# Down projection of a SwiGLU as seven quarter products, with weight sums made by GpSimd beforehand

## What is computed

```python
D_MODEL = 2048; SEQ = 512; N_MEM = 256; FFN_HIDDEN = 5632

def swiglu(h, w_gu, w_down):
    g, u = jnp.split(h @ w_gu, 2, axis=-1)
    return (jax.nn.silu(g) * u) @ w_down

def reference(x, mem, positions, ...):
    h = rmsnorm(x, norm_mix_g)
    ...                       # two attention mixers, o_a and o_b
    x = x + (gates[:, :, 0] * (o_a @ w_branch_a) + gates[:, :, 1] * (o_b @ w_branch_b)) @ w_out
    x = x + memory_cross_attention(rmsnorm(x, norm_cross_g), rmsnorm(mem, norm_mem_g), w_xq, w_xkv, w_xo)
    hf = rmsnorm(x, norm_ffn_g)
    x = x + swiglu(hf, w_gu, w_down)
    return rmsnorm(x, final_norm_g)
```

## Time and profile before

| what | us |
|---|---|
| median of 3 runs (2743.96 to 2745.4) | 2745.27 |
| the profiled execution's own span | 2743.1 |
| start to the first mix matmul | 1409.7 |
| mix stage | 829.3 |
| down stage | 488.8 |
| from the last piece to the end | 15.3 |

### The profile page before, as it was taken

The page is one execution under the profiler, slowest core; times in us unless marked ns, Lnnn a source line. Parts: engine busy times, 40 slices in busy tenths (PEclk is TensorE's granted clock), DMA queues, the critical chain, the costliest instruction groups (busy, mean ns, idle before and its releaser), DMA issues.

```text
span 2743.1 us, 34950 instructions
## 1 busy us (share of the span) xinstructions
PE 2704.5 (99%) x13710; PEld 2279.2 (83%) x13710; DVE 1737.1 (63%) x1820; ACT 1017.7 (37%) x1134; POOL 766.3 (28%) x642
## 2 busy tenths in 40 slices
PE   9999999999999999999999999999999999999997
PEld 7888888888778888888788888888888888888886
DVE  6677652334653344573677767687777777777786
ACT  6555432224642232243553333333333332222224
POOL 0000000000000003330357666776667632212120
PEclk9999999999999999999999999999999999999999
DMA  6221233322222325333434444434343463444432
GB/s 239 77 85 62 83 97 99 92 84 92 77 93 92 99 77 207 93 121 109 139 109 137 132 138 132 138 101 146 127 143 127 143 238 123 161 146 137 161 125 82
DMA packets 125889, 333.29 MB, mean 121 GB/s; under 512 B 10320, under 2 KB 57424, under 8 KB 125136
## 3 DMA queue, kind: packets, MB, share of 16 engines
q1 hardware_dynamic: 119296, 309.37, 35.3%
q10 hardware_dynamic: 6480, 22.35, 2.0%
HBM read 301.27 MB, written 30.41 MB: 121 GB/s over the span
## 4 chain that ended last, share of the span: by engine, by line
PE 92%; DVE 4%; ACT 1%; DMA 1%; issue 1%; SPq 0%; DVEq 0%; ACTq 0%
PE ps L2198 16%; PE acc L1812 14%; PE acc L1814 14%; PE acc L1813 14%; PE ps L2201 8%; PE acc L1832 6%; PE acc L1834 6%; PE acc L1833 6%; PE acc L2198 3%; PE acc L2201 1%; DMA x_tokens<-x_n 1%; PE ps L1874 1%; PE ps L1863 1%; DVE w_lo L1588 1%; ACT ps L799 0%
## 5 line engine op out<-in xcount | busy, mean ns | idle before, releaser
L1101 DVE TENSOR_TENSOR w_lo<-raw,w_hi 128x1024 fp32r<-128x1024 f32 x328 | 475.9, 1456 | 274.9 <-ACT w_hi L609 274.3
L1812 PE MATMUL acc<-act_both,w_hi 128*128 128x512 f32 (+1 forms) x1536 | 591.1, 385 | 3.6 <-DVE w_lo L1101 3.1
L1814 PE MATMUL acc<-act_both,w_lo 128*128 128x512 f32 (+1 forms) x1536 | 585.3, 381 | 0.0
L1813 PE MATMUL acc<-act_both,w_hi 128*128 128x512 f32 (+1 forms) x1536 | 584.9, 381 | 0.0
L609 ACT ACTIVATE w_hi<-raw 128x1024 fp32r<-128x1024 f32 x328 | 344.3, 1055 | 553.9 <-PE acc L1814 340.7
L1812 PEld LDWEIGHTS acc<-act_both,w_hi 128*128 128x128 f32 x1536 | 289.6, 189 | 59.4 <-DVE w_lo L1101 3.7
L1814 PEld LDWEIGHTS acc<-act_both,w_lo 128*128 128x128 f32 x1536 | 289.5, 188 | 55.4
L1813 PEld LDWEIGHTS acc<-act_both,w_hi 128*128 128x128 f32 x1536 | 289.8, 189 | 54.3 <-issue 0.7
L543 POOL MEMSET mem_stat<- 128x256 f32 x1 | 0.3, 312 | 1047.1 <-DMA mem<-mem_t 1047.1
L2198 PE MATMUL ps<-t_both,w_hi 128*128 128x512 f32 x896 | 281.6, 396 | 0.5 <-DVE cg L1616 0.5
L1832 PE MATMUL acc<-act_both,w_hi 128*128 128x512 f32 x672 | 262.9, 391 | 3.1 <-DVE x L1456 3.0
(11 more groups left out here) (306 smaller groups left out, 4752.8 us busy)
## 6 DMA issues: line engine op xcount, KB each, us to landing
raw<-w_stream SPq DMA_DIRECT2D x412, 512.0 KB, 3.6
over<-w_stream SPq DMA_DIRECT2D x84, 512.0 KB, 4.4
gate_t<-cg ACTq DMA_DIRECT2D x22, 512.0 KB, 2.6
over<-gate_t SPq DMA_DIRECT2D x22, 512.0 KB, 5.3
up_t<-cu ACTq DMA_DIRECT2D x20, 512.0 KB, 2.6
over<-up_t SPq DMA_DIRECT2D x20, 512.0 KB, 6.2
x<-x_t SPq DMA_DIRECT2D x16, 512.0 KB, 8.6
x_tokens<-x_n SPq DMA_DIRECT2D x4, 1024.0 KB, 15.4
```

Of the source, the lines that this page charges most:

```text
L1101: nc.vector.tensor_tensor(w_lo[:, s, :], raw[:, s, :], f(w_hi[:, s, :]), ALU.subtract)\
L1812: nc.tensor.matmul(dst, wh, ah, start=start and k == 0, stop=False)
L1813: nc.tensor.matmul(dst, wh, al, start=False, stop=False)
L1814: last = nc.tensor.matmul(dst, wl, ah, start=False, stop=stop and k == UK - 1)
```

## The change

The down projection is cut into quarters as the mix stage already was: hidden features (22 tiles each half, so pair p is now made of tiles p and p + 22), tokens (256 each half), outputs (8 tiles each half). Seven quarter products follow each other, each of 22 units. A unit has eight output tiles with three matmuls of 256 columns, into eight half banks of PSUM, and `x` is added to at the end of each product (`down_out`). Four of the products need sums of weight quarters. GpSimd makes these in 88 steps during the two gate stages: SyncE loads a step (512 KB, rows of 1 KB), GpSimd runs four operations of 256 elements, SyncE stores the sums to DRAM (512 KB). SwiGLU is finished within the mix stage for every pair (as the inline pairs were), with the token and feature sums of the hidden tiles made by VectorE, and eight quarters of a pair are stored (1 MB). The mix stage uses half banks of 256 columns too: each weight tile pair takes three matmuls of 256 columns instead of 512 + 256 (two tiles: 6 x 256 for 2 x 512 + 2 x 256), a group is read from PSUM by VectorE with five operations instead of ten, and TensorE waits once per group for its bank set. In the last product the output tile is the outer loop, so that `x` is finished one tile after another, and GpSimd adds up the squares.

```diff
-MIXES = (FFN // P - DIRECT) // 2
+MIXES = HID_PAIRS - 1
 MIX_UNITS = 8
 U_MIX = U_FFN + 4 * DIRECT
 U_DOWN = U_MIX + MIX_UNITS * MIXES
-UNITS = U_DOWN + GROUPS * KT // 2
+DOWNS = 7
+UNITS = U_DOWN + DOWNS * HID_PAIRS
...
+SCALED = [(1, 0, 4), (1, 4, 8), (1, 8, 12), (1, 12, 16), (0, 0, 4), (0, 4, 8), (0, 8, 12), (0, 12, 14), (0, 14, 16)]
...
+Q21, Q11, Q12, Q22 = range(4)
+W_QUADS = U_DOWN
+W_LAST = W_QUADS + 4 * HID_PAIRS
...
+DOWN_PRODUCTS = ((Q11, H11), (Q12, H21), (SUM2, HT2), (SUM1, HT1), (SUM3, HT3), (SUM4, H22), (Q22, HT4))
...
+SUM_COLS = 256
+SUM_STEPS = HID_PAIRS * UK * P // SUM_COLS
+SUM_BUFS = 3
+SUM_UNITS = (range(U_DB + 8, U_SWA), range(U_DA + 8, U_OUT))
...
+        def half_bank(bank_set, i):
+            at = 4 * S * bank_set + SH * i
+            return banks[:, at:at + SH]
...
-            ring(2, U_OUT // RING + 1)
+            def sums_in_(t):
+                if t >= SUM_BUFS:
+                    sp.wait_ge(sums_out[t % SUM_BUFS], 16 * (t // SUM_BUFS))
+                k, c = divmod(t, UK * P // SUM_COLS)
+                quads = w[W_QUADS:W_LAST, :, SUM_COLS * c:SUM_COLS * (c + 1)].rearrange("(q k) p c -> k p q c", q=4)
+                sp.dma_start(sums[t % SUM_BUFS][:], quads[k]).then_inc(sums_in[t % SUM_BUFS], 16)
+            def sums_out_(t):
+                k, c = divmod(t, UK * P // SUM_COLS)
+                sp.wait_ge(down_summed, t + 1)
+                sp.dma_start(down_sums[:, k, :, SUM_COLS * c:SUM_COLS * (c + 1)].rearrange("q p c -> p q c"),
+                             sums[t % SUM_BUFS][:]).then_inc(sums_out[t % SUM_BUFS], 16)
+            def with_sums(units):
+                begun = sums_due(units[0]).start
+                for n in units:
+                    weights(n)
+                    if n == units[0]:
+                        sp.wait_ge(ps_free, 2 + 2 * PAIRS + (0 if n < U_SWA else SWA_STEPS))
+                    for t in sums_due(n):
+                        sums_in_(t)
+                        if t > begun:
+                            sums_out_(t - 1)
+                sums_out_(sums_due(units[-1]).stop - 1)
+            ring(2, SUM_UNITS[0].start // RING)
+            with_sums(SUM_UNITS[0])
+            ring(U_SWA // RING, SUM_UNITS[1].start // RING)
+            with_sums(SUM_UNITS[1])
...
+            for t in range(SUM_STEPS):
+                part = sums[t % SUM_BUFS]
+                pool.wait_ge(sums_in[t % SUM_BUFS], 16 * (t // SUM_BUFS + 1))
+                link(nc.gpsimd.tensor_tensor(part[:, SUM3, :], part[:, Q21, :], part[:, Q11, :], ALU.subtract))
+                link(nc.gpsimd.tensor_tensor(part[:, SUM1, :], part[:, Q21, :], part[:, Q22, :], ALU.add))
+                link(nc.gpsimd.tensor_tensor(part[:, SUM2, :], part[:, SUM3, :], part[:, Q22, :], ALU.add))
+                nc.gpsimd.tensor_tensor(part[:, SUM4, :], part[:, Q12, :], part[:, SUM2, :], ALU.subtract)\
+                    .then_inc(down_summed, 1)
...
+            def gate_mixed(p):
+                pool.wait_ge(sig_made, p + 1)
+                nc.gpsimd.tensor_tensor(cg[:], cg[:], sig, ALU.mult).then_inc(hid_mixed, 1)
...
+            def store_hidden(p):
+                act.wait_ge(hid_made, p + 1)
+                act.dma_start(hid_t[:, :, p, :].rearrange("j p s -> p j s"), hid[:]).then_inc(hid_stored, 16)
+            def sigmoid_of(p):
+                if p:
+                    act.wait_ge(hid_stored, 16 * p)
+                act.wait_ge(gate_scaled, p + 1)
+                nc.scalar.activation(sig, cg[:], ACT.Sigmoid).then_inc(sig_made, 1)
...
+            def read_products(g, out):
+                b = mix_set(g)
                 both_tiles = [P, 2, SH]
-                dve.wait_ge(products_done, len(TOLD) * g + 1)
-                link(nc.vector.tensor_copy(out[:, 1, :], half(0, 1)))
-                link(nc.vector.tensor_tensor(out[:, 1, :], half(0, 0), out[:, 1, :], ALU.add))
-                dve.wait_ge(products_done, len(TOLD) * g + 2)
-                added(out[:, 0:4:3, :], out[:, 1:2, :].broadcast_to(both_tiles), lambda h: two_banks(0, h), freed)
-                dve.wait_ge(products_done, len(TOLD) * g + 3)
-                added(out[:, 1:3, :], out[:, 3:4, :].broadcast_to(both_tiles), lambda h: two_banks(1, h))
-                added(out[:, 3, :], out[:, 2, :], lambda h: half(3, h), freed)
-                between()
                 dve.wait_ge(unit_done, U_MIX + 4 * (g + 1))
-                added(out[:, 1:3, :], out[:, 1:3, :], lambda h: two_banks(2, h), freed)
-            read = Tally()
+                link(nc.vector.tensor_copy(out[:, 1, :], half_bank(b, 0)))
+                link(nc.vector.tensor_tensor(out[:, 0:4:3, :], two_products(b, 1),
+                                             out[:, 1:2, :].broadcast_to(both_tiles), ALU.add))
+                link(nc.vector.tensor_tensor(out[:, 1:3, :], two_products(b, 3),
+                                             out[:, 3:4, :].broadcast_to(both_tiles), ALU.add))
+                link(nc.vector.tensor_tensor(out[:, 3, :], half_bank(b, 3), out[:, 2, :], ALU.add))
+                nc.vector.tensor_tensor(out[:, 1:3, :], two_products(b, 5), out[:, 1:3, :], ALU.add)\
+                    .then_inc(products_read, 1)
...
+            def make_hidden(p):
+                dve.wait_ge(hid_mixed, p + 1)
+                link(nc.vector.tensor_tensor(cu, cu, cg[:], ALU.mult))
+                link(nc.vector.tensor_tensor(hid[:, HT1:HT3 + 1, :], hid[:, H12:H12 + 1, :].broadcast_to([P, 2, SH]),
+                                             hid[:, H11:H22 + 1:3, :], ALU.subtract))
+                link(nc.vector.tensor_tensor(hid[:, HT2, :], hid[:, H11, :], hid[:, HT3, :], ALU.subtract))
+                nc.vector.tensor_tensor(hid[:, HT4, :], hid[:, H21, :], hid[:, HT2, :], ALU.subtract)\
+                    .then_inc(hid_made, 1)
...
+                read_gate(p)
+                mix_low()
+                scale_gate()
+                if p < MIXES:
+                    mix_low(3)
+                    read_up(p)
                     mix_low()
-                    dve.wait_ge(up_stored, 16 * UPS_STORED[p - 1])
-                    nc.vector.tensor_tensor(cg[:], cg[:], both, ALU.mult).then_inc(gate_scaled, 1)
-                    dve.wait_ge(sig_made, INLINE.index(p) + 1)
-                    link(nc.vector.tensor_tensor(cg[:], cg[:], cu[:], ALU.mult))
-                else:
+                    scale_up()
                     mix_low()
...
+                    make_hidden(p)
+                    mix_low(2)
...
-                    dst = bank(g % 2, at)
-                    if c == 0 and g and at in FREED_BY:
-                        pe.wait_ge(products_read, READ_STEPS * (g - 1) + FREED_BY[at])
+                    dst = half_bank(mix_set(g), at)
                     src = act_both if kind == "b" else t_both
                     for j in range(2):
-                        nc.tensor.matmul(dst, hi[:, w_block, P * j:P * (j + 1)], src[:, :, ks.start + 2 * c + j, toks],
-                                         start=c == 0 and j == 0, stop=False)
-                    for j in range(2):
-                        last = nc.tensor.matmul(dst[:, SH:S], lo[:, w_block, P * j:P * (j + 1)],
-                                                src[:, 1, ks.start + 2 * c + j, toks], start=False,
-                                                stop=c == 3 and j == 1)
-                    if c == 3 and at in TOLD:
-                        last.then_inc(products_done, 1)
+                        k = ks.start + 2 * c + j
+                        wh, wl = (t[:, w_block, P * j:P * (j + 1)] for t in (hi, lo))
+                        nc.tensor.matmul(dst, wh, src[:, 1, k, toks], start=c == 0 and j == 0 and at % 2 == 0, stop=False)
+                        nc.tensor.matmul(dst, wh, src[:, 0, k, toks], start=False, stop=False)
...
+            def down_product(i):
+                if i < 2:
+                    pe.wait_ge(products_read, 2 * MIXES - 1 + i)
+                else:
+                    pe.wait_ge(down_read, i - 1)
+                for k in range(HID_PAIRS):
+                    pe.wait_ge(lo_done, u.at(1))
+                    if k % PIECE == 0:
+                        pe.wait_ge(hid_lo, DOWN_PIECES * i + k // PIECE + 1)
+                    for m in range(UK):
+                        wh, wl = (t[:, u.n % RING, P * m:P * (m + 1)] for t in (w_hi, w_lo))
+                        last = three(half_bank(down_set(i), m), wh, wl, *down_tile(i, k), k == 0 and m % 2 == 0,
+                                     k == HID_PAIRS - 1 and m % 2 == 1)
+                    last.then_inc(unit_done, 1)
+                    u.add()
...
```

644 lines of the change are left out of this document (313 added, 331 removed).

## The result

The changed kernel takes 2812.88 us (median of 4 runs, 2807.41 to 2816.82), the kernel before 2745.34: a ratio of 1.0244, interval 1.0229 to 1.0259, so 2.4% slower. Forecast were 2727, with 8 chances in 10 for 2716 to 2750. All times here are of undisturbed executions; one of the two of the run no_steps (2980.9 us, at a granted clock of 0.83) was disturbed and is left out.

The account below looks back on a forecast made before the run. TensorE's matmul stream was taken to bound the kernel. 2743.1 + 21.2 (mix) - 38.9 (down) - 1.1 (tail) = 2724.3 us of span, 2726.5 as median, stated as 2727; 8 in 10 for 2716 to 2750.

Parts of the forecast that it names:

- The matmuls: Mix stage: 42 groups of 168 matmuls at 120.0 ns take 846.7 us; with small waits 850.5, 21.2 us slower.
- the down stage: 3696 matmuls at 120.0 ns take 443.5 us; with entry and other waits 449.9, 38.9 us faster.
- the tail: Behind the last matmul: one scaling of four tiles moves ahead of it, 1.1 us faster.
- Rival E: Matmuls of 256 columns follow each other faster than 120.0 ns; 2698 to 2719 us; chance 0.05.
- D: Down stage: each product change starves TensorE by 2.5 us, six times; 2742 us; chance 0.06.
- The prediction's other time, about 2698: From the Trainium skill's matmul price, 109.2 ns for 256 columns: mix stage loses 6 us, down stage gains 52.
- so I cost all this at nothing: Mix stage: work of VectorE and GpSimd beside the matmuls stays hidden behind TensorE's 5.04 us per unit; 0 us.
- the term of GpSimd: Mix stage: GpSimd has 8 x 3.3 + 3 = 29 of 40.3 us per pair.
- Rival C: VectorE bounds the mix stage, TensorE waiting about 2 us per pair; 42 us, 2769; chance 0.07.
- rival B: Gate stages: sum steps hold back weights at SyncE's wait for `down_summed`; (step - 5.35) x 86, up to 2783; chance 0.15.
- (1.0 + L + P) / 2: Gate stages: time per sum step from load landing L, 5.1, and four GpSimd operations P, 3.7; 4.9 us.
- what is allowed: Gate stages: unit 95's load may go out until 593, so 42 steps may take 5.39 us each; 5.35 used.

Follow-up runs that it names:

- no_steps: The changed kernel without the 88 sum steps; products that want sums read plain weight quarters; 2766.47 us.
- pool_half: The changed kernel with sums of every second mix unit and the gate product on VectorE, stores of sums issued by GpSimd; 2784.98 us.
- pool_store: The changed kernel with the stores of the sums issued by GpSimd instead of SyncE; 2822.45 us.
- weights_last: The changed kernel with the load of a sum step issued ahead of the weight unit in SyncE's queue; 2801.79 us.
- late_store: The changed kernel with the sums of a step stored one step later by SyncE; 2836.49 us.

## Why the prediction was wrong

**The matmuls, the down stage, the tail: right, with two terms that cancel.** In the down stage matmuls start 120 ns apart. Its entry has waits of 1.1 and 2.2 us ahead of the third and the fifth unit (1.0 and 2.5 were walked out), and the product changes cost nothing. The 2.9 us for `hid_lo` waits and the norm's stream did not come (0.3 at most), and some 1.5 for matmuls at half clock behind the second wait, which no term had, did. So 449.3 against 449.9 is in part luck. Rival E is out, D too. The prediction's other time, about 2698, leaves out the 10 us of waits that its own sum adds (3.8 and 6.4); with them it is 2708.

**The mix stage: the step "so I cost all this at nothing" failed, in the term of GpSimd.** I gave it 8 x 3.3 + 3 = 29 us of a pair's 40.3. The 3.3 per unit lay between its three operations undisturbed, 2.9 with gaps, and their means in the stage before, 3.5 to 3.7. No reason was given for taking the undisturbed end. Measured are 5.05 per unit (5.85 where the unit lies in `raw`, 4.25 where in `over`) and 42.5 per pair, 893.1 / 21. The old means were taken beside the old VectorE, and they hide two kinds of operations, 0.74 us and 1.29, as counted above. The change rebuilds VectorE's work: its ten reads of PSUM per group, beside which GpSimd takes 0.74, become five, and six operations of 256 to 1024 elements on two SBUF operands per pair come in. In the stretch counted above VectorE's operations on two SBUF operands fill 520 of 740 us, where it was 331. I counted VectorE's load (79% forecast, 83% measured) and not what kind of work it was. Rival C had the size, 42 us, but the wrong engine: with VectorE at 94% (pool_half) the stage loses 4 us, with GpSimd never idle 46.

The Trainium skill says as much on the page "SBUF — State Buffer", section "Who interferes with whom": a VectorE instruction with two SBUF inputs and a GpSimd instruction that reads SBUF take turns, each holding the shared interface to its end, and one with at most one SBUF input, outside the 2-port perf modes, doesn't contend. The trace agrees on both sides, 2.4 to 2.5 us beside splits and 0.74 beside PSUM reads. The prediction had the same contention from the Trainium skill, but weighed it for the steps of the gate stages alone, at 0.22 us per operation from the mean of the stage before, and not for the mix stage, where it decides.

**The gate stages: rival B, with chance 0.15, is what happened.** Its place and the formula for a step, (1.0 + L + P) / 2, were right; the mechanism was right in part, since without SyncE's wait for `down_summed` (pool_store) a step still takes 5.56. The sizes were off. L is 6.0 us and not 5.1, P is 4.0 and not 3.7. That gives 5.5, and 5.43 is measured, with 4.9 forecast. I had let one transfer, the weight unit, hold up the load, and the store of the step before is ahead of it too. But the number of transfers ahead doesn't give L either: in weights_last only the store is ahead, and L is 6.1. What the runs show is that fewer bytes (5.0) and longer rows (5.4) shorten it; what share of it each transfer has stays open.

The second error is in what is allowed, and without it little would have been lost: by rival B's own price a step of 5.43 costs (5.43 - 5.35) x 86 = 7 us, and 46 were lost. I took unit 95 as the last that matters, behind 42 steps and needed at 599.1 for its matmuls. It is unit 96. It goes out behind the stores of all 44 steps, and it has to be split before VectorE reads the bank that unit 95's matmuls want at 599.1, though its own matmuls come 5.4 us later. So (599.1 - 6 - 366.6) / 45 = 5.03 us a step are allowed, where I used 5.35. Then (5.43 - 5.03) x 45 = 18 us, and landing, rounding and splitting of unit 96 take 7.8 instead of 6, in a burst of four units: 19.8. Unit 95's matmuls start at 619.1, 20.0 later than before, and 2.8 more go to the matmuls at half clock behind that. The stage loses 22.9. That the 56 us of the prediction's upper bounds come near is luck: they belong to a step of 6.0.

**The chances.** The gate stages' failure was rival B, the mix stage's had no rival of its own: no case had GpSimd late there. Both came from the same omission, a cost taken near its undisturbed value beside a resource that the change itself makes busier. With the allowed step counted right, 5.03, it lies in the middle of the range of steps that I gave (4.2 to 6.0), and rival B would have had a chance near one half in place of 0.15.

## What to carry to other kernels

Sort an engine's operations by what they read and write before adding up its load: work moved from PSUM reads to SBUF operands raised VectorE's load here only from 74 to 83%, and GpSimd's time for a unit's sums by some 40% (3.5 to 3.7 us became 5.05). Where a queue waits for a step of load, compute and store, price the step by landings under the traffic that the change makes (here 6.0 us against 4.1), and measure before relying on another order. With rows of 1 KB three other orders gave 5.26 to 5.68 us for 5.43, with rows of 4 KB one of them gave 4.85 for 5.21. Fewer bytes and longer rows moved the step each time. Look up when the last item of such a series is due, and for whom: a queue that works in order can need it for an instruction that doesn't read it, as VectorE's read of a bank behind a split. When a wait is put down to an instruction that looks unrelated, look at what stands ahead of that instruction in its queue.

## What was unexpected of the hardware

- Each of the six waits of TensorE of 3.9 to 8.1 us in the gate stages of the changed kernel was followed by 7 to 13 matmuls at the half clock level, 1.5 to 2.8 us more each. Of its twelve waits of 1.4 to 1.9 us in the mix stage seven were followed by a stretch at that level. In all 23.9 us went this way in the gate and mix stages, about a quarter of what they lost to waits and clock.
- Three transfers of 512 KB issued in a row landed after 4.4, 5.3 and 6.0 us (late_store), where the median of the weight loads in the kernel before is 3.5 in the gate stages and 4.1 in the mix stage. In the changed kernel's order they took 3.4, 4.9 and 6.0. In both the last one came 7.0 us after the first was issued, in the order of weights_last 7.9.
- Halving the operations of GpSimd cut its busy time in the mix stage by 63% (855 to 320 us). More of them then overlap no VectorE operation on two SBUF operands (50 of 151 of those with 256 elements, where it was 69 of 277), and the others take 1.27 us on average instead of 1.84.
